# A two-layer streaming encoder on one core: the first column chunk of the input projection taken by tokens, in two passes

## The reference

```python
shift, scale, gate = jnp.split(ada_mod(c, ada_w, ada_b), 3, axis=-1)      # silu(c) @ ada_w + ada_b
h = rms_norm(x, norm_g) * (1 + scale[:, None, :]) + shift[:, None, :]
q, k, v, g = jnp.split(h @ w_in, [1024, 2048, 4096], axis=-1)
q = rotary(q.reshape(b, L, 4, 256), pos)
k = rotary(k.reshape(b, L, 4, 256), pos) * 256 ** -0.5
...
return x + gate[:, None, :] * (o @ w_out), r
```

## Time and profile before

| | us |
|---|---|
| median of three runs | 1756.92 |
| lowest and highest of them | 1753.44 and 1757.35 |
| the profiled execution, its own time | 1755.21 |
| its span, from the first to the last instruction | 1753.4 |
| TensorE busy in the span | 1700.9 |
| mean granted TensorE clock | 0.997 |

### The profile page before, as it was taken

One profiled execution on the slowest core, in us unless ns is written; L12 is line 12 of the kernel. 1 busy time (PEld: TensorE's weight loads), 2 busy tenths in 40 slices (PEclk: granted clock), 3 DMA queues, 4 the chain that ended last, 5 costly groups with the idle time before them and its releaser, 6 DMA issues.

```text
span 1753.4 us, 22335 instructions
## 1 busy us (share of the span) xinstructions
PE 1700.9 (97%) x8585; PEld 1344.2 (77%) x8585; DVE 751.1 (43%) x1561; ACT 564.1 (32%) x926; POOL 382.8 (22%) x501
## 2 busy tenths in 40 slices
PE   3999999999999999999999999999999999999998
PEld 2899997777876766667678888888788877778876
DVE  4654442212244445555533334745553016544432
ACT  4311121111134444444431224425222135444442
POOL 2111111211133333342332224404200000110000
PEclk9999999999999999999999999999999999999999
DMA  9535445563466767667661311332322736432201
GB/s 306 180 139 177 164 151 201 171 219 131 170 183 186 238 209 227 182 221 251 212 232 58 111 36 37 112 122 80 100 85 88 214 116 193 133 106 73 73 25 37
DMA packets 137002, 260.73 MB, mean 149 GB/s; under 512 B 16931, under 2 KB 60095, under 8 KB 136898
## 3 DMA queue, kind: packets, MB, share of 16 engines
q1 hardware_dynamic: 104114, 167.23, 30.4%
q0 software_dynamic: 32784, 92.08, 15.5%
HBM read 178.83 MB, written 80.43 MB: 148 GB/s over the span
## 4 chain that ended last, share of the span: by engine, by line
PE 86%; DVE 4%; issue 2%; DMA 2%; ACT 2%; POOL 0%; SPq 0%; DVEq 0%; POOLq 0%; ACTq 0%
PE trunk_ps L1105 35%; PE in_ps_o L533 12%; PE in_ps_o L529 11%; PE tail_ps L1983 6%; PE tail_ps L1974 4%; PE tail_ps L1941 3%; PE trunk_ps L1148 3%; PE trunk_ps L1132 2%; PE tail_ps L1951 2%; DVE room L1538 1%; PE trunk_ps L1209 1%; PE in_ps_o L554 1%; PE tail_ps L1917 1%; PE trunk_ps L1143 1%; DMA out_state_prompt<-room 1%
## 5 line engine op out<-in xcount | busy, mean ns | idle before, releaser
L1105 PE MATMUL trunk_ps<-w_hi,hT_hi 128*128 128x512 f32 x1008 | 410.8, 408 | 0.0
L1105 PE MATMUL trunk_ps<-w_hi,hT_lo 128*128 128x512 f32 x1008 | 401.7, 399 | 0.0
L1105 PE MATMUL trunk_ps<-w_lo,hT_hi 128*128 128x512 f32 x1008 | 397.9, 395 | 0.0
L1105 PEld LDWEIGHTS trunk_ps<-w_hi,hT_hi 128*128 128x128 f32 x1008 | 189.8, 188 | 59.2 <-issue 17.6
L1105 PEld LDWEIGHTS trunk_ps<-w_lo,hT_hi 128*128 128x128 f32 x1008 | 189.7, 188 | 49.8 <-issue 5.0
L1105 PEld LDWEIGHTS trunk_ps<-w_hi,hT_lo 128*128 128x128 f32 x1008 | 189.6, 188 | 44.5
L208 DVE TENSOR_TENSOR w_lo<-w_raw,w_hi 128x1024 fp32r<-128x1024 f32 x76 | 96.5, 1271 | 114.7 <-ACT w_hi L196 109.3
L529 PE MATMUL in_ps_o<-hT_hi,w_hi 128*128 128x384 f32 x384 | 131.4, 342 | 3.2 <-DVE hT_lo L656 3.2
L529 PE MATMUL in_ps_o<-hT_hi,w_lo 128*128 128x384 f32 x384 | 129.7, 338 | 0.0
L529 PE MATMUL in_ps_o<-hT_lo,w_hi 128*128 128x384 f32 x384 | 129.7, 338 | 0.0
L533 PE MATMUL in_ps_o<-w_hi,hT_hi 128*128 128x512 f32 x288 | 114.4, 397 | 0.0
(11 more groups left out here) (243 smaller groups left out, 2862.9 us busy)
## 6 DMA issues: line engine op xcount, KB each, us to landing
w_raw<-in_a_w_in SPq DMA_DIRECT2D x96, 256.0 KB, 3.3
room<-in_state_ret SPq DMA_DIRECT2D x64, 256.0 KB, 4.2
out_state_sample<-room POOLq DMA_DIRECT2D x64, 256.0 KB, 6.7
room<-in_b_ada_w SPq DMA_DIRECT2D x24, 512.0 KB, 6.6
scratch_qkT<-room POOLq DMA_DIRECT2D x48, 192.0 KB, 2.2
scratch_v_hi<-room POOLq DMA_DIRECT2D x36, 256.0 KB, 2.6
scratch_v_lo<-room POOLq DMA_DIRECT2D x36, 256.0 KB, 3.1
scratch_o<-room POOLq DMA_DIRECT2D x36, 256.0 KB, 3.3
```

The lines of the kernel that those rows point to most:

```text
L1105: ins = pe.matmul(ps[:, bank, :], h[:, k, t * P:(t + 1) * P], w[:, (C0 + j) % 2, k, :], start=k + m == 0, stop=k == KT - 1 and m == 2)
```

## The change

The tokens are now taken in two groups. The first pass takes tiles 0 to 2 (384 tokens), in step with the conditioning blocks; the second takes tiles 3 to 8 (640 prompt and 128 stream tokens).

- SP loads tokens in three groups of three tiles, the second and third behind conditioning blocks 2 and 3. The cosine and sine tables go to another place and are loaded when the last conditioning rows are out.
- In the first chunk a tile number now means other columns and tokens (`where`): tiles 0 to 3 are the four column blocks of the first 384 tokens, 4 to 7 of the next 384, 8 to 11 of the last.
- The first pass transposes three tiles a block, modulates, copies and subtracts 384 tokens, and adds to tiles 0 to 3. ScalarE squares tiles 3 to 8 between its copies, VectorE scales groups two and three late in the pass.
- Behind the first pass ScalarE copies tiles 0 to 3 out. The second pass transposes six tiles a block, works on 768 tokens, and adds to tiles 4 to 7 (tokens 384 to 767), in the same four PSUM banks.
- Tiles 8 and 9 use two further banks. Tile 8's is the bank of the side products, so the first side product waits until that tile is copied out (`evac` at 9).
- GpSimd's first splits wait for the first group of tokens alone. The next chunk's weights are split at tiles 2 to 5.
- In `tail` the gate rows are loaded inside the loop, before the seventh head of the first step, behind loads of values and queries.

```diff
+    def where(c, t):
+        return (t % 4 // 2, t // 4, t % 2) if c == 0 else (t // 6, t % 6 // 2, t % 2)
+
     def bank(c, t):
+        if c == 0 and t in (2 * AHEAD, 2 * AHEAD + 1):
+            return AHEAD + (t - 2 * AHEAD)
         return t % 4 if c < ROT else t % 3
...
-    early = [0, 1, 3, 4]
+    early = [2, 3, 4, 5]
...
-        ps_t = ps("ps_t", [P, 3, 512])
-        ps_o = ps("ps_o", [P, 5, 512])
+        ps_o = ps("ps_o", [P, 8, 512])
+        ps_t = ps_o[:, 5:8, :]
...
+        spans = [slice(0, 3 * P), slice(3 * P, TOKENS)]
...
-            for t in range(TILES):
-                sp.dma_start(xv[:, t], x_rows(t)).then_inc(x_in[t // 3], 16)
+            x_group(0)
             load_sub(pr, sp, chunks[0], 0, 0)
             load_sub(pr, sp, chunks[0], 0, 1)
             ada_block(1)
             ada_block(2)
+            x_group(1)
             load_sub(pr, sp, chunks[0], 0, 2)
             ada_block(3)
             load_sub(pr, sp, chunks[0], 0, 3)
+            x_group(2)
             load_parts(pr, sp, chunks[1], 1, 0)
-            sp.wait_ge(h_ready, KT)
+            sp.wait_ge(*rows_out[3])
             sp.dma_start(cs[:, 0], pr.table["cos"]).then_inc(tab_landed, 16)
             sp.dma_start(cs[:, 1], pr.table["sin"]).then_inc(tab_landed, 16)
+            sp.wait_ge(h_ready, 2 * KT)
             side_load(0)
...
-            for t in range(TILES):
+            for t in range(3):
                 squares(t)
-                if t in (3, 6):
-                    root(t // 3 - 1)
-            root(2)
+            root(0)
             for sub in range(2):
                 split_hi(pr, act, 0, 0, sub)
             for d in range(KT):
-                act.wait_ge(ht_ready, d + 1)
-                act.copy(hT_hi[:, d, :], ht[:, d % 2, :]).then_inc(hi_done, 1)
-                if d in (2, 4):
-                    split_hi(pr, act, 0, 0, 1 + d // 2)
-            act.wait_ge(h_ready, KT)
+                high(0, d)
+                if d in (3, 5):
+                    g = (d - 1) // 2
+                    split_hi(pr, act, 0, 0, 1 + g)
+                    squares(3 * g)
+                    squares(3 * g + 1)
+                if d in (4, 6):
+                    g = (d - 2) // 2
+                    squares(3 * g + 2)
+                    root(g)
+            high(1, 0)
+            for n in range(AHEAD):
+                evacuate(n)
+            for d in range(1, KT):
+                high(1, d)
+            act.wait_ge(h_ready, 2 * KT)
...
                     if r == 0:
                         pe.wait_ge(side_tab, 5 * 16)
-                        pe.wait_ge(*mods_out[3])
+                        pe.wait_ge(evac, 2 * AHEAD + 1)
...
             for m in range(4):
-                turn(2 * m)
+                turn(0, 2 * m)
                 if m:
-                    step(2 * m - 1)
-                turn(2 * m + 1)
+                    step(0, 2 * m - 1)
+                turn(0, 2 * m + 1)
                 if m < 3:
                     ada(m + 1)
-                step(2 * m)
+                step(0, 2 * m)
                 if m < 3:
                     fold_rows(m + 1)
-            step(KT - 1)
+            turn(1, 0)
+            step(0, KT - 1)
+            for d in range(KT):
+                if d + 1 < KT:
+                    turn(1, d + 1)
+                step(1, d)
...
-            for g in range(3):
-                scaled_rows(g)
+            mean(0)
+            scaled_rows(0)
             for m in range(4):
-                modulated(2 * m)
-                low(2 * m)
-                modulated(2 * m + 1)
+                modulated(0, 2 * m)
+                low(0, 2 * m)
+                if m in (2, 3):
+                    mean(m - 1)
+                modulated(0, 2 * m + 1)
                 if m < 3:
                     rows(m + 1)
-                low(2 * m + 1)
+                else:
+                    scaled_rows(2)
+                low(0, 2 * m + 1)
                 if m < 3:
                     mods(m + 1)
+                if m == 2:
+                    scaled_rows(1)
+            modulated(1, 0)
+            for d in range(KT):
+                low(1, d)
+                if d + 1 < KT:
+                    modulated(1, d + 1)
```

More of the change, by code:

```diff
@@ L281, in intake @@
         tmp = part_of_x(2 * CW).rearrange("p (s c) -> p s c", s=2)
-        cs_flat = part_of_x(2 * TOKENS)
-        cs = cs_flat.rearrange("p (s c) -> p s c", s=2)
+        spare = part_of_x(2 * TOKENS)
+        cs = xs
         side_bias = part_of_x(3 * CW)[0:4].rearrange("p (r c) -> p r c", r=3)
@@ L355, in ada_block, with x_group @@
                                      dr["a_ada_w"][rows, cols].rearrange("(k p) c -> p k c", p=P)).then_inc(ada_in[m % 2], 16)
+            def x_group(g):
+                for t in range(3 * g, 3 * g + 3):
+                    sp.dma_start(xv[:, t], x_rows(t)).then_inc(x_in[g], 16)
             chunks = weights + [after]
@@ L415, in _ @@
                     if c < ROT:
-                        part, col, half = t // 6, t % 6 // 2, t % 2
+                        part, col, half = where(c, t)
                         pool.wait_ge(rotated, 2 * (tile_no(c, t) // 2) + half + 1)
@@ L452, in _, with high, evacuate @@
             act.activation(c_silu, c_rows, ACT.Silu).then_inc(rooted, 1)
-            for t in range(TILES):
+            def high(s, d):
+                act.wait_ge(ht_ready, KT * s + d + 1)
+                act.copy(hT_hi[:, d, spans[s]], ht[:, d % 2, spans[s]]).then_inc(hi_done, 1)
+            def evacuate(n):
+                act.wait_ge(out_done, n + 1)
+                act.copy(stage[:, n, 0:NB3], ps_o[:, n, 0:NB3]).then_inc(evac, 1)
+            for t in range(3):
                 squares(t)
-                if t in (3, 6):
-                    root(t // 3 - 1)
-            root(2)
+            root(0)
             for sub in range(2):
@@ L475, in _ @@
                         act.copy(side_c[:, q % 2, :, :], pr.cT[:, 2 * (q % 4):2 * (q % 4) + 2, :]).then_inc(side_c_ready, 1)
[L476 to L479, removed]
+                    if n >= AHEAD:
+                        act.wait_ge(out_done, n + 1)
+                    if c < ROT and n >= AHEAD:
+                        act.wait_ge(rotated, 2 * ((n - 4) // 2) + 2)
                         act.copy(stage[:, s, 0:NB3], ps_o[:, bank(c, t), 0:NB3]).then_inc(evac, 1)
-                    else:
+                    elif c >= ROT:
                         m = TILES * (c - ROT) + t
@@ L510, in fold_rows, with turn @@
                 ins.then_inc(ada_done, 1)
-            def turn(d):
+            def turn(s, d):
                 if d == 0:
[L515 to L519, removed]
+                    for g in ((0,), (1, 2))[s]:
+                        pe.wait_ge(*x_scaled[g])
+                if s + d:
+                    pe.wait_ge(ht_ready, KT * s + d)
+                for i in range((3, 6)[s]):
+                    ins = pe.transpose(ps_t[:, i // 4, (i % 4) * P:(i % 4 + 1) * P], xv[:, 3 * s + i, d * P:(d + 1) * P], pr.ident[:, :])
                 ins.then_inc(turned, 1)
@@ L525, in products @@
                 if c < ROT:
-                    part, n, half = t // 6, t % 6 // 2, t % 2
+                    part, n, half = where(c, t)
                     w0 = part * DK + half * P
@@ L565, in side_end, with step @@
                 ins.then_inc(side_turned, 1)
-            def step(d):
-                pe.wait_ge(h_ready, d + 1)
+            def step(s, d):
+                pe.wait_ge(h_ready, KT * s + d + 1)
                 pe.wait_ge(pr.raw_split, d // KS + 1 + 2)
-                for t in range(AHEAD):
+                for t in range(AHEAD * s, AHEAD * (s + 1)):
+                    if s and d == 0:
+                        pe.wait_ge(evac, t - AHEAD + 1)
                     products(0, t, d)
@@ L610, in _, with mean @@
         def _(dve):
-            def scaled_rows(g):
+            def mean(g):
                 part = slice(3 * g, 3 * g + 3)
@@ L615, in scaled_rows @@
                 dve.tensor_scalar(stat[:, 1, part], stat[:, 0, part], 1.0 / D, EPS, ALU.mult, ALU.add).then_inc(prepared, 1)
+            def scaled_rows(g):
+                part = slice(3 * g, 3 * g + 3)
                 dve.wait_ge(*root_of[g])
@@ L685, in _ @@
                     if c < ROT and t % 2:
-                        n = t % 6 // 2
+                        n = where(c, t)[1]
                         m = tile_no(c, t)
@@ L1865, in _ @@
                 load_sub(pr, sp, pr.last_weight, C0 + 1, sub)
-            for b in range(DEC_BATCH):
-                sp.dma_start(gate_s[DEC_SEQ * b:DEC_SEQ * (b + 1), :], dr["gate"][1, b:b + 1, :].to_broadcast([DEC_SEQ, D])).then_inc(gate_in, 16)
-            sp.dma_start(gate[:, :], dr["gate"][1, DEC_BATCH:, :].to_broadcast([P, D])).then_inc(gate_in, 16)
             for s in range(STEPS):
                 for i in range(FH):
+                    if s == 0 and i == 6:
+                        for b in range(DEC_BATCH):
```

(2 more changed lines are left out.)

51 lines of the change are left out of this document (28 added, 23 removed).

## The result

| | before | after |
|---|---|---|
| median on the same chip, us | 1755.18 (4 runs) | 1763.14 (4 runs) |
| ratio, with its 95% interval | | 1.0053 [1.0039, 1.0066] |
| the profiled execution, own time and span, us | 1755.21, 1753.4 | 1763.84, 1762.0 |
| the twelfth tile's copy starts at, us | 113.14 | 122.90 |

A forecast was written before the change was run, and what follows sets the result against it. TensorE, busy 97% of the span, was taken as the bound. Its terms, 81.7 + 16.5 + 2.85 + 12.8 + 2.1 = 116.0 against 113.1, gave 2.8 us later: 1758.0 us, with 8 in 10 for 1749 to 1763.

The forecast's parts named there:

- the mark: Start of the twelfth tile's copy in the first column chunk, 113.14 us before; forecast 116.0, the difference carried to the end.
- The first pass starts earlier: Start of the program: three scaled tiles suffice, so transposes start at 23.4 us, 7.2 ahead of 30.64.
- How long it lasts: First pass until the fourth conditioning block is folded: 21.9 us of TensorE work plus 0.6, 1.1 and 1.0, ending at 48.0.
- The loads allow it: Third token group's load, behind 15.2 MB: through at 49.4 us at 308 GB/s or 43.7 at 348; ScalarE wants it at 49.
- second rival: Slower case: third token group comes at 51.5 us, 2.4 after ScalarE wants it; 5.0 more, 1763.0 us; chance 0.29.
- From there VectorE leads: Behind the fourth block's fold, VectorE's chain of scalings and modulations takes 8.1 us; last tokens scaled at 56.1.
- The second pass: Loop of VectorE and ScalarE over 768 tokens: 3.1 us each, eight loops 24.8, last subtraction at 81.7, 8.9 later than before.
- What waits then: Side product behind the ninth tile waits for that tile's copy, 16.5 us after the second pass; TensorE stands 10.1, ends 9 to 13.
- The restart: TensorE's slower clock after the stand at the side product: 2.1 us, ends 0 and 2.85.
- The gate loads of the last stage: Gate loads moved behind values and queries in the last stage: gain taken as 0, ends -1.7 and +0.5 us.
- TensorE's own pace: Faster rival: first pass runs at this pace, second pass ends at 76.6; 1750.8 us, or 1749.1 with the last stage; chance 0.19.
- Covering the new wait: Third rival, at the side product: the new wait is covered after all, 9.4 us less, 1745.8 us; chance 0.05.

The follow-up runs named there:

- e2_later_slot: The changed kernel with the first side product behind the twelfth tile instead of the ninth; 1752.83 us, ratio 0.9993 to the kernel before.
- e4_scale_early: The changed kernel with VectorE scaling the second token group ahead of the fourth conditioning rows' bias; 1762.49 us, ratio 1.0043 to the kernel before.

## Why the prediction was wrong, step by step

It had the right chain and the right place of the loss, and left the mark 6.9 us short (122.9 for 116.0): 4.1 at the end of the second pass, 2.0 in front of the side product and 0.8 in the restart.

- **The first pass starts earlier**: right. Transposes at 22.95, forecast 23.4.
- **How long it lasts**: wrong, and here most was lost. The fourth block was folded at 51.75, not 48.0. The step that failed is "The loads allow it". It asked only when the third token group lands. The fourth conditioning block is wanted first, at 42, and stands behind 8.4 MB of conditioning (itself included), 3.1 MB of tokens and 1.6 MB of weights. These 13.1 MB need 42.6 us at the 308 GB/s that the prediction itself used; with the 2 us until a landing is seen that its second rival adds, 44.6. It was 45.23. The sum has nothing for this landing; measured, it is a wait of 3.10, and the block behind it took 3.44 instead of 1.92. The 1.0 for VectorE beside GpSimd's splits was not paid by TensorE: a subtraction took 1.25 instead of 0.56 once (up to 2.75 in the runs), and TensorE had other work.
- **The second rival, loads that spend the lead**: its mechanism was right, its victim was another load, and that its price of 1763.0 comes so near to 1763.14 is luck: it was worked out for the third token group, and 2.8 of the 6.9 us come from elsewhere. The third group was first used at 50.57, later than the 49 from which it was to decide, but did not decide: VectorE's own chain was later still, as the run that scaled early shows.
- **From there VectorE leads**: right. Last tokens scaled at 59.64, 7.9 behind the fold, forecast 8.1. The run that scaled early moved the end of the pass by 1.9.
- **The second pass**: right in pace (loops of 3.11 to 3.19, forecast 3.1); 26.2 from the scaled tokens to the last subtraction against 25.6. It ended at 85.84, and 81.7 was forecast, nearly all of it from the late fold.
- **What waits then**: the mechanism was right, the size 2.0 short. From 85.84 to the end of the copy 18.5 us pass, forecast 16.5. The step that failed is "the third split waits some 0.6 for its weights": VectorE waited 2.82. The weights were issued at 90.44 and converted at 96.72, so the load took 6.3, the whole 6.2 of its row, which the prediction had named as its upper end. The stand of 12.09 lies in its 9 to 13. The late weights were not tried by themselves; the runs with later splits move them and the splits together.
- **The restart**: 2.1 was taken from the transposes and the block of before; it cost 2.9 (122.90 - 104.35 - 2.85 - 12.8), just above the upper end of 2.85; 2.5 of it are the side product's own (5.4 for 2.85). The rows show the lower clock, granted 0.50 and 0.52, in the stretches around the side product. The Trainium skill (TensorE: Matmul & The Clock Gate, "Part 1: The HAM clock gate") says that an array left idle falls to the half clock and that activity brings it back; here the trace agrees, in the clock column too.
- **The gate loads of the last stage**: right in the reason, that VectorE is late next, and 0.7 us short in the size. The term was put at 0; the cold stretch behind the two waits, which goes with them, was not thought of. It lies within the stated ends and works against the rest of the error.
- **The other rivals**: TensorE's own pace was not reached, since the loads came late. Covering the new wait takes other splits and another place of the side product, as the runs show; in the changed kernel it is not covered.

Behind the mark the changed span is 1.2 us shorter than that of before, and 0.7 of this is the last stage. In the eight experiments this rest (behind the side product, where that stands last) lies between 1636.6 and 1643.3, and is 1640.3 before, so no cause is looked for in what is left. Not tried was another order of the loads: the bytes ahead of the third token group, which landed near 50.6, are the same in any order, and how much of the wait for the fourth block could be had so stays open.

## What to carry to other kernels

When a load order is changed, add up the bytes ahead of every transfer that something waits for, not of the last one alone. Before a wait is added in front of a piece of work, ask whether that work must stand there: moving the side product three tiles on cost nothing and gave more than freeing its bank. A long wait covers others (a table, a small copy, a store); taking it away shows them, so price the next in line before hoping for the whole of it.

## What was unexpected in the hardware

- The start of the program differs between executions: TensorE's first work came at 11.5 us in the changed kernel and at 13.9 in the run with the banks. The end of the second pass hardly moved with it (85.84 and 85.36), since the fourth conditioning block landed at 45.2 and 46.2: an execution that starts later waits less for it.
- A shorter stand did not mean a shorter cold stretch. Worked out as above, the restart cost 2.9 behind 12.09 us of standing in the changed kernel, 2.6 behind 12.00 and 3.8 behind 11.99 in the runs that scaled early and left out the load, and 3.85 behind 7.47 in the run with later splits. The fourth block took 3.43 behind a wait of 2.34 (e2_later_slot) and 2.74 behind one of 2.54 (e4_scale_early). So one profile fixes such a term only to about 1 us.
